# A relative bias table from one product with eight rows, stored with each row repeated 128 times

## The reference, cut to what matters

```
dist = q_pos[:, None] - k_pos[None, :]
bias = rel_bias[t5_causal_bucket(dist)].astype(jnp.float32).transpose(2, 0, 1)
s = einsum('bhcqd,bhckd->bhcqk', q_blk, kt) + bias[None, :, None]
s = where(dist >= 0, s, -inf)
```

## Time and profile before

| | us |
|---|---|
| median of 3 runs | 1515.35 (1514.86 to 1516.71) |
| profiled execution, its own time | 1513.05 |
| its span | 1511.4 |
| TensorE busy | 1421.0 |
| VectorE busy | 1064.6 |
| ACT busy | 693.0 |
| POOL busy | 203.1 |
| DMA, mean rate | 221 GB/s |

### The profile page before, as it was taken

How to read it: one execution, slowest core, us unless ns; L and a number is a source line. 1 busy time by engine, 2 the same in 40 slices (tenths; PEclk the granted TensorE clock), 3 DMA queues, 4 the chain that set the end, 5 groups by cost and what they waited for, 6 DMA issues and landing times.

```text
span 1511.4 us, 19404 instructions
## 1 busy us (share of the span) xinstructions
PE 1421.0 (94%) x6936; PEld 1181.5 (78%) x6936; DVE 1064.6 (70%) x1103; ACT 693.0 (46%) x903; POOL 203.1 (13%) x295
## 2 busy tenths in 40 slices
PE   5987899999699999999899999999999897899998
PEld 5886778888588887768788887888879886688887
DVE  5897857776578885685667775688866978555554
ACT  2543444333444444665644345444447654444442
POOL 3102301110301111321201103011110000100000
PEclk8996899999799999999999999999999998899999
DMA  9844568997389993433589972999934332256661
GB/s 356 300 171 147 177 221 300 312 311 259 116 287 344 337 319 124 167 111 112 180 267 312 317 257 91 311 342 348 326 114 166 121 131 84 73 192 222 215 229 70
DMA packets 187348, 334.01 MB, mean 221 GB/s; under 512 B 9129, under 2 KB 123405, under 8 KB 187168
## 3 DMA queue, kind: packets, MB, share of 16 engines
q1 hardware_dynamic: 160528, 237.95, 46.9%
q0 software_dynamic: 26560, 95.13, 17.6%
q10 hardware_dynamic: 208, 0.23, 0.0%
HBM read 330.65 MB, written 2.62 MB: 221 GB/s over the span
## 4 chain that ended last, share of the span: by engine, by line
PE 80%; DVE 9%; ACT 4%; issue 2%; POOL 2%; DMA 1%; SPq 0%; DVEq 0%; ACTq 0%; POOLq 0%
PE ps L2006 70%; PE ps L2444 2%; PE ps L2120 2%; PE ps L2183 1%; DVE wlo L1215 1%; PE ps L2112 1%; ACT whi L638 1%; DVE ada_acc L1493 1%; DMA big<-in_w_ada 1%; ACT hf L645 1%; POOL st L551 1%; PE ps L2656 1%; DVE ada_acc L1887 1%; POOL st L488 1%; PE ps L2542 1%
## 5 line engine op out<-in xcount | busy, mean ns | idle before, releaser
L1215 DVE TENSOR_TENSOR wlo<-raw,whi 128x2048 fp32r<-128x2048 f32 x215 | 490.7, 2285 | 152.7 <-ACT whi L638 151.1
L2006 PE MATMUL ps<-whi,hhi 128*128 128x512 f32 (+1 forms) x1208 | 492.0, 407 | 21.4 <-DVE hlo L1263 15.7
L638 ACT ACTIVATE whi<-raw 128x2048 fp32r<-128x2048 f32 x215 | 409.9, 1910 | 204.4 <-PE ps L2006 174.5
L2006 PE MATMUL ps<-whi,hlo 128*128 128x512 f32 (+1 forms) x1208 | 478.1, 396 | 0.0
L2006 PE MATMUL ps<-wlo,hhi 128*128 128x512 f32 (+1 forms) x1208 | 478.1, 396 | 0.0
L2006 PEld LDWEIGHTS ps<-whi,hhi 128*128 128x128 f32 x1208 | 232.5, 192 | 76.7 <-issue 20.1
L2006 PEld LDWEIGHTS ps<-whi,hlo 128*128 128x128 f32 x1208 | 231.5, 192 | 50.2
L2006 PEld LDWEIGHTS ps<-wlo,hhi 128*128 128x128 f32 x1208 | 232.7, 193 | 45.8 <-issue 1.0
L2006 PE MATMUL ps<-whi,ahi 128*128 128x512 f32 x400 | 159.5, 399 | 0.0
L2006 PE MATMUL ps<-wlo,ahi 128*128 128x512 f32 x400 | 158.5, 396 | 0.0
L2006 PE MATMUL ps<-whi,alo 128*128 128x512 f32 x400 | 158.4, 396 | 0.0
(11 more groups left out here) (278 smaller groups left out, 1423.8 us busy)
## 6 DMA issues: line engine op xcount, KB each, us to landing
raw<-in_ffn_w_in SPq DMA_DIRECT2D x176, 512.0 KB
ada_raw<-in_ada_w POOLq DMA_DIRECT2D x96, 512.0 KB, 5.1
raw<-in_ffn_w_down SPq DMA_DIRECT2D x44, 1024.0 KB
big<-in_ada_w POOLq DMA_DIRECT2D x48, 512.0 KB, 6.1
ada_raw<-in_w_ada POOLq DMA_DIRECT2D x32, 512.0 KB, 5.2
raw<-in_hgrn_w_in SPq DMA_DIRECT2D x16, 1024.0 KB
raw<-in_attn_w_qkv SPq DMA_DIRECT2D x12, 1024.0 KB
raw<-in_w_gate SPq DMA_DIRECT2D x22, 512.0 KB
```

The lines of the kernel that those rows point to most:

```text
L638: sc.activation(whi[:, slot, 0:n], raw[:, slot, 0:n], ACT.Copy).then_inc(w_hi, 1)
L1215: ve.tensor_tensor(wlo[:, slot, 0:n], raw[:, slot, 0:n], whi[:, slot, 0:n].bitcast(F32), ALU.subtract)\
L2006: done = pe.matmul(dst, lhsT, rhs, start=first and n == 0, stop=final and n == 2, skip_group_check=True)
```

## The change

POOL no longer copies the columns and no longer waits there for its two loads; TensorE waits for them itself. The 33 x 8 matrix is the stationary operand of one product, with eight rows out, into bank 7. One copy of 8 x 384 takes it to `big`. TensorE does not wait for the copy. The store reads eight partitions, each row 128 times (a step of 0), with the heads as the outermost dimension of both sides. The skewed read is as it was.

```diff
--- before.py
+++ after.py
@@ -578,10 +578,6 @@
                         pool.memset(big[0:BUCKETS + 1, 2440:2448], NEG).then_inc(toe_fill, 1)
                         pool.wait_ge(toe_fill, 1)
                         pool.dma_start(big[0:BUCKETS, 2440:2448], rel_bias_2[:, :]).then_inc(toe_land, 16)
-                        pool.wait_ge(toe_land, 32)
-                        pool.tensor_copy(big[0:BUCKETS + 1, 2560:3584].rearrange("b (h q) -> b h q", h=HEADS),
-                                         big[0:BUCKETS + 1, 2440:2448].unsqueeze(2).to_broadcast((BUCKETS + 1, HEADS, P)))\
-                            .then_inc(toe_fill, 1)
 
                     ada_pieces(s)
                 if s == 0:
@@ -596,9 +592,9 @@
                         early_piece(n)
                 elif s == 1:
 
-                    pool.wait_ge(toe_rows, HEADS)
-                    pool.dma_start(bias_rows[:, :, :], big[:, 3584:3584 + HEADS * TOE].rearrange("p (h j) -> p h j", h=HEADS))\
-                        .then_inc(toe_land, 16)
+                    pool.wait_ge(toe_rows, 1)
+                    pool.dma_start(bias_rows.rearrange("p h j -> h p j"),
+                                   big[0:HEADS, 2560:2560 + TOE].unsqueeze(1).to_broadcast((HEADS, P, TOE))).then_inc(toe_land, 16)
                     pool.wait_ge(toe_land, 48)
                     skewed = bass.AP(tensor=bias_rows.tensor, offset=bias_rows.offset + P - 1,
                                      ap=[[HEADS * TOE - 1, P], [TOE, HEADS], [1, TOK]])
@@ -745,10 +741,8 @@
                 hi(U + 3)
                 body(U + 2, 1)
                 if s == 1:
-                    for h in range(HEADS):
-                        sc.wait_ge(toe_mm, h + 1)
-                        sc.activation(big[:, 3584 + h * TOE:3584 + (h + 1) * TOE], ps[:, 6 + h % 2, 0:TOE], ACT.Copy)\
-                            .then_inc(toe_rows, 1)
+                    sc.wait_ge(toe_mm, 1)
+                    sc.activation(big[0:HEADS, 2560:2560 + TOE], ps[0:HEADS, 7, 0:TOE], ACT.Copy).then_inc(toe_rows, 1)
                 with sc.Fori(2, NCH - 1) as i:
                     body(U + 5, i, i - 2)
                 body(U + 3 * (NCH - 1) - 1, NCH - 1, more=False)
@@ -2208,14 +2202,10 @@
                 body(U + 2, 1, first_down=True)
                 if s == 1:
 
-                    pe.wait_ge(toe_fill, 2)
+                    pe.wait_ge(toe_land, 32)
                     pe.wait_ge(cols_set, 2)
-                    for h in range(HEADS):
-                        if h >= 2:
-                            pe.wait_ge(toe_rows, h - 1)
-                        pe.matmul(ps[:, 6 + h % 2, 0:TOE], big[0:BUCKETS + 1, 2560 + h * P:2560 + (h + 1) * P],
-                                  big[0:BUCKETS + 1, 2048:2048 + TOE], start=True, stop=True).then_inc(toe_mm, 1)
-                    pe.wait_ge(toe_rows, HEADS)
+                    pe.matmul(ps[0:HEADS, 7, 0:TOE], big[0:BUCKETS + 1, 2440:2448], big[0:BUCKETS + 1, 2048:2048 + TOE],
+                              start=True, stop=True).then_inc(toe_mm, 1)
                 with pe.Fori(2, NCH - 1) as i:
                     body(U + 5, i, i - 2)
                 last = U + 3 * (NCH - 1) - 1
```

## The result

The changed kernel takes 1520.7 us (median of 8 runs, 1518.92 to 1523.94), the kernel before beside it 1515.09 (8 runs, 1509.45 to 1520.83). The ratio is 1.0032, 95% interval 1.0016 to 1.0048: slower by about 5 us. The forecast was 8.8 us faster. The time lies within the range, 0.3 us from its upper end, and close to what one rival gave for 34 us of store (1521).

A forecast was written before the change was run, and what follows sets the result against it. It took TensorE, busy 94% of the span, as the bound. Products 7.6 plus clock 1.5 less store 0.3 made 8.8 us, from the median 1515.35 to 1506.5; range 1504.5 to 1521.

The forecast's parts named there:

- one rival: Store at the end of sublayer 1 slower than two engines' pace: 1521 at 34 us, about 1546 at 59; chance 0.19.
- The eight products, 7.62 us: At the table, one product of 0.65 us replaces eight, so TensorE goes on at 208.16 instead of 215.78: 7.62 us gained.
- The clock, 1.5 us: Behind the table, TensorE's clock stays up because no gaps between products are left: 1.5 us gained, bounds 0 and 1.5.
- The next units are ready: Behind the table, the weight units TensorE takes next are ready seven microseconds sooner, so no new wait: cost 0.
- POOL's copy at nothing: POOL loses a 1.03 us copy and a 1.34 us wait; later loads come 2.4 us sooner, counted as 0.
- Eight engines: The store is cut along its outer dimension, the eight heads, so eight engines take 0.197 MB each: at least 7.4 us.
- the store's price: Store at the end of sublayer 1: 7.4 to 59 us of transfer, landing taken as 15 to 19 us, charged 0.3.
- The two rivals with a slow store: Late weights at the end of sublayer 1: store gives most or all back, 1510 to 1518 (0.33), or is slower (0.19).
- The rival built on it: Partitions 0 to 7 give two engines' pace, a 29.5 us store; weights late, time about 1516; chance 0.33.
- transfer of 28.4 us: Store length at which the late first weight unit of the next block cancels the 9.1 gained; each further microsecond is lost.
- POOL's root: Layer-norm root, POOL's next work after the skewed read, at 374.32 after 24 us idle; a landing up to 35 us hides.
- Sum: Whole kernel: 7.6 for the products plus 1.5 for the clock, less 0.3 for the store, 8.8 us faster.

The follow-up runs named there:

- stride of two: Changed kernel with the heads in partitions 0, 2, ... 14 (16 rows out of the product), the store reading those: 1506.88 us, ratio 0.9953.
- stride of four: Changed kernel with columns copied four times on POOL, 32 rows out, the store reading partitions 0, 4, ... 28: 1503.37 us, ratio 0.9911.
- both from 128 rows: Changed kernel with 128 rows out, stored from all partitions: each row eight times, 1501.41 us; or once, with eight skewed reads of 16 partitions, 1501.4 us.
- the old kernel with the same source: Kernel before the change, eight products kept; its store reads only partitions 0 to 7, each 12 KB row sixteen times: 1532.93 us, ratio 1.0116.
- the half store: Changed kernel storing 64 copies of each row instead of 128, from partitions 0 to 7, with two skewed reads of 64 partitions: 1513.2 us, ratio 0.9981.

## Why the prediction was right or wrong

- **The eight products, 7.62 us.** Right: 7.53 on the timeline. A product with eight rows out costs TensorE what one with 128 does, 484 and 483 ns a record.
- **The clock, 1.5 us.** Right: 1.00 in the window behind. Both terms together were 9.1 in the forecast, and 8.6 to 9.0 in the part of the kernel up to the last modulation piece, in the change and in the kernels whose store hides.
- **The next units are ready.** Right: fifteen products in the 3.3 us behind the table, the loop full.
- **POOL's copy at nothing.** Right: up to the last modulation piece the kernels that still copy the columns on POOL (stride of two, stride of four, both from 128 rows) gain 8.6 to 9.0, those without the copy 8.6 to 8.9.
- **Eight engines.** Right: the slow packets hold 6.4 engines on the mean in the change and 7.4 in the old kernel with the same source, and the landing of 17.1 us with a stride of four is that of eight engines at their own pace in the forecast. The Trainium skill, DMA: Bandwidth & Descriptors (rules for kernel authors), warned of an outermost dimension below 16. The runs agree that it confines the store, but that alone cost nothing here.
- **The step that failed is the store's price: "for the forecast I take eight engines at their own pace".** I had put both ends down, 7.4 and 59 us, and taken the first because the old store was the nearest row by bytes. It was not the nearest by source: it read 128 partitions. The two rivals with a slow store had 0.52 together, more than the forecast's 0.42. In place of the 7.4 us the packets took about 31 (by their records), and the landing 35.4 where I had 15 to 19. The rule that spoke against it was in the text: the Trainium skill, SBUF — State Buffer (door 1, the DMA port swizzle), puts partitions 0 to 3 on one port and 4 to 7 on another, at 27.2 GB/s each. The runs agree: 24.5 GB/s for one group, 50 for two, and an engine's own pace from a stride of four. The rival built on it gave 29.5 us for the transfer, which is near.
- **Who pays, and from when.** The rivals had the mechanism right, packets of weights that wait for their turn on held engines, and three things wrong. They named the first unit of sublayer 2 as the late one; in the change the last down unit of sublayer 1 is on the chain, and ACT's wait of 1.6 us for the unit that I named comes on top without delaying the end. (In the old kernel with the source 0 to 7, in the half store and with the stride of two the chain does go through that unit.) They left out the clock, 2.8 us behind the gap. And the "transfer of 28.4 us" as the point from which it decides was too late: the half store, with some 14 us of packets, already loses, in part at least by the store itself. I had let only the time count at which the store ends, as if weights flowed at their full need until then. The rows say 107 GB/s for 30 us, against 210 in the same stretch of the kernel before. That the time comes near the 1521 which the slower rival gave is partly luck: that was for a transfer of 34 us, and for the 31 measured its sum gives 1518.
- **POOL's root.** "A landing up to 35 us after issue hides" stands, and never came to a test: even at 65.1 us VectorE's moments came later.
- **Sum.** In place of 9.1 - 0.3 the profile has 8.6 - 15.6 = -7.0 from marker to marker; by the runs the change loses 5 us. The ratio's interval, 2.4 to 7.3, holds both. The profiled execution is 3.0 us shorter behind the root, within what that stretch varies by among the profiles.

## What to carry to other kernels

A transfer's price goes by the partitions that it reads, not by its bytes alone: a small source that is repeated with a step of 0 saves work on the compute engines and can quadruple the time on the DMA engines. When few rows must be the source, lay them four partitions apart (tried here for partitions 0 to 28), or let one product write 128 rows, since a record took 483 ns with 128 rows out and 484 with eight. And a slow transfer is a tax on the other queue that uses the same engines: price it by how long each of its packets holds an engine beside the stream that must not starve, and not by whether its own landing is waited for. Where the late load makes TensorE stand, add what the lower clock costs behind the gap, 2.8 us here.

## What the runs showed of the hardware

- Four engines that read four neighbouring partitions get a quarter of their pace each, exactly in the packets: 1.86 us for 12 KB against 0.46. Two in a group get more than half (17.9 of 25 to 27 GB/s). I take it that each of them spends part of its time on packets of weights; that was not tried.
- SP's own issue of a load was stretched while the engines were held: 3.56 and 3.57 us for the two norm rows (L473) in the change, 4.07 and 3.45 in the half store, against 0.82 and 0.69 with a stride of four. In the half store's chain these two issues are 7.5 us on the path themselves.
- The slow store of 12 KB packets lost a little more than that of 4.6 KB (17.6 against 15.6 us, at about the same landing); whether by the longer hold of a packet was not tried by itself.
- Two skewed reads of 64 partitions held the engines for 84 engine-microseconds where one of 128 held them for 48, for 1.0 MB. Eight reads of 16 partitions held them for 72 for 0.78 MB (337 to 345 of that kernel). That is 21, 12 and 11 GB/s on a held engine: the narrower the reads, the slower. I had not expected that, and no run tells why.
- TensorE's granted clock in the gap of 12.8 us was 0.69 and 0.61 in the 7 us behind it, where twelve products took 5.08 us in place of 2.75.
